# Gate matrix by two fp32r products per token, and one half of the context network's gate and up slabs split

## The chip, the cores and the metric

The kernel runs on one NeuronCore of one Trainium2 chip. The metric is device microseconds of one execution, and lower is better. The time before is the median of 3 runs.

## The reference, cut to what matters

The model is two blocks in a row. Its first ends with a product-key expert layer, and its second runs a stream of 512 tokens beside a context of 256 tokens, with modulated norms, mixers and gated feed-forward networks (silu of a gate times an up product, then a down product). The part that the change touches is this:

```python
experts = (i1 * PEER_NKEYS + i2).reshape(t, PEER_HEADS * PEER_TOPK)      # 128 of 16384 experts per token
gates = jax.nn.softmax(cv, axis=-1).reshape(t, PEER_HEADS * PEER_TOPK)
...
act = jax.nn.gelu(jnp.einsum('tkd,td->tk', expert_u[eb], xb))
out = jnp.einsum('tk,tkd->td', act * gb, expert_v[eb])
```

and, for the context, `(silu(x @ w_gate) * (x @ w_up)) @ w_down` with a hidden width of 22 slabs of 128.

## The kernel before, in words

**Products.** Most products are made in fp32r (a 32-bit format that TensorE takes in one pass) from an upper and a lower part of both operands: upper by upper, upper by lower, lower by upper, three products in place of one. ScalarE writes the upper part of a weight slab of 128x1024 (line 522), and VectorE or GpSimd the lower part (line 530), slabs in three buffers, at most two slabs ahead. A `direct` unit takes the slab and the activations whole in float32, one product per block of 128 rows (line 555, the first two slabs of a network at line 573); it needs no split, and no engine but TensorE.

**The context network** (`cnet`, class `Network`) handles 256 tokens. Its hidden width is in two halves of 11. Each half has 22 gate and up slabs and then 11 down slabs. All 66 slabs are direct. Its input comes from `cffn` (class `Apply`): VectorE scales 8 blocks, and ScalarE adds the shift to each (line 731, signal "moved").

**The dense gate matrix.** The first 384 tokens are handled densely: every expert slab is multiplied with all of them, and the gates of all other experts are zero. For each token, the 128x128 matrix of its gates is the product of two one-hot matrices over the token's 128 choices, one for each half of the expert number, one of them scaled by the gates. The stream `dense` works in 96 steps of GT = 4 tokens, and is three steps deep. In step k VectorE makes both one-hot matrices of tokens 4k to 4k+3 (line 3458), in the step after that ScalarE (4 operations, line 3469, even groups) or GpSimd (one operation, line 3486, odd groups) multiplies the gates in, and in step k+3 TensorE makes 4 float32 products of 128x128x128 (line 3443). ScalarE copies the result to a stage (line 3477), and the DMA queue of SyncE writes every fourth stage to DRAM (line 3494). Once all are written, the gates of each group of 8 slabs are loaded (`gates_sync`, line 3518). The dense steps need the chosen experts of their tile of 128 tokens, which the stream `route` finds on VectorE.

**The order** of the instructions on each engine is laid down when the kernel is built, by a planner (`Weave`). It keeps a clock for each engine, charges every operation a cost by a formula, and puts a step of a side stream in when the signals that its TensorE part needs are expected to have come and when the backlog of the engines that the step before used is over. The charges that matter here:

```python
if rhs.dtype == F32R:
    self.spent += max(n / 2400 + 0.013, 0.058)
else:
    self.spent += max(n * 0.00168, 0.14) * (1.0 if out.shape[0] > 64 else 0.55)
...
fixed, rate = {"vector": (0.14, 0.00106), "scalar": (0.14, 0.00089), "gpsimd": (0.35, 0.00205)}.get(self.name, (0, 0))
```

Where a stage ends with `plan.drain()`, all side steps that are left are put in before the spine goes on. After `cnet` come the 13 slabs of the context mixer `cm1` (split, lower parts on GpSimd), then such a drain, then `gates 1`, the start of the stream `experts`, and the 256 peer slabs of 384 tokens (split on ScalarE and VectorE).

**The experts stream** handles the last 128 tokens by fetching rows. GpSimd issues indirect DMAs (line 3646) of 128 rows of 4 KB into five buffers, VectorE multiplies and sums each (lines 3604 and 3618), in 257 steps that are due every 3.96 us of the planner's TensorE clock. The first step issues the first five fetches and holds the first VectorE operation. At the end TensorE transposes the sum (line 3593).

## Time and profile before

| | |
|---|---|
| median of 3 runs | 3975.88 us (3972.86 to 3977.01) |
| profiled execution, its own time | 3978.74 us |
| its span in the trace | 3976.9 us |
| granted TensorE clock, mean | 0.983 of 2.4 GHz |
| TensorE (PE) busy | 3823.1 us, 96% |
| VectorE (DVE) busy | 2328.4 us, 59% |
| ScalarE (ACT) busy | 1570.5 us, 39% |
| GpSimd (POOL) busy | 693.6 us, 17% |

Times are microseconds from the start of the span. Each float32 product stands in the trace as two records of PE and two of PEld (weight load), and each fp32r product as one of each. The duration of a PE record includes its latency, so what a product costs in a dense row of products is the distance from one start to the next. "us" of a merged row reaches from the first start to the last end.

### The profile page before, as it was taken

What the parts mean: (1) busy time and instruction counts of PE and PEld (TensorE: products, weight loads), DVE (VectorE), ACT (ScalarE), POOL (GpSimd) and SP (SyncE); (2) the same over time, 40 slices, a digit from 0 to 9 for tenths busy, and PEclk for the clock granted to TensorE, in tenths of its full rate; (3) what the DMA queues carried; (4) which work ended last, traced back from release to release, by engine and by line L of the source; (5) the groups of instructions that cost most, each with busy time, mean ns of one, the idle gap of its engine ahead of it and who ended that gap; (6) DMA issues with size and microseconds to landing.
All of it is one profiled execution on the core that took longest, in us unless ns stands there. A gap on an engine that the chain in (4) does not pass through costs nothing.

```text
span 3976.9 us, 55816 instructions
## 1 busy us (share of the span) xinstructions
PE 3823.1 (96%) x22529; PEld 3304.4 (83%) x22529; DVE 2328.4 (59%) x4053; ACT 1570.5 (39%) x2531; POOL 693.6 (17%) x586
## 2 busy tenths in 40 slices
PE   8999999989999989999999999998899999889998
PEld 5788776778899889999999999786677777667887
DVE  6455333546888467777777776557633345664333
ACT  4523342444345543333333333536522233564222
POOL 0112000244112343222233221201100010101000
PEclk9999999999999999999999999998999999999999
DMA  5211235533355678888888886312234342203332
GB/s 207 81 41 44 102 118 200 177 99 99 108 176 198 212 238 294 289 277 284 274 283 283 285 285 196 113 55 62 82 118 136 122 143 69 74 26 87 99 97 75
DMA packets 209184, 617.19 MB, mean 155 GB/s; under 512 B 18464, under 2 KB 68640, under 8 KB 205088
## 3 DMA queue, kind: packets, MB, share of 16 engines
q1 hardware_dynamic: 168352, 465.76, 36.6%
q0 software_dynamic: 40576, 147.87, 10.8%
q8 instruction: 179, 2.93, 0.3%
q14 instruction: 77, 0.63, 0.1%
HBM read 583.67 MB, written 29.88 MB: 154 GB/s over the span
## 4 chain that ended last, share of the span: by engine, by line
PE 85%; DVE 7%; ACT 4%; DMA 2%; issue 2%; POOL 0%; SPq 0%; DVEq 0%; ACTq 0%; POOLq 0%
PE ps L598 22%; PE ps L609 21%; PE ps L600 21%; PE ps L555 6%; PE ps L3443 2%; PE ps L2513 1%; DMA raw<-w_in 1%; PE ps L2540 1%; PE ps L887 1%; DVE hlo_plain L764 1%; ACT whi L522 1%; PE ps L2121 1%; PE ps L2531 1%; PE ps L1218 1%; PE ps L1209 1%
## 5 line engine op out<-in xcount | busy, mean ns | idle before, releaser
L598 PE MATMUL ps<-hhi,whi 128*128 128x512 f32 (+1 forms) x2824 | 1075.9, 381 | 6.8 <-DVE xres L3049 2.9
L600 PE MATMUL ps<-hlo,whi 128*128 128x512 f32 (+1 forms) x2824 | 1048.8, 371 | 0.1
L530 DVE TENSOR_TENSOR wlo<-raw,whi 128x1024 fp32r<-128x1024 f32 x543 | 671.3, 1237 | 635.6 <-ACT whi L522 628.2
L522 ACT ACTIVATE whi<-raw 128x1024 fp32r<-128x1024 f32 x594 | 625.7, 1054 | 601.7 <-PE ps L609 452.8
L609 PE MATMUL ps<-hhi,wlo 128*128 128x512 f32 (+1 forms) x2824 | 670.3, 376 | 9.0 <-DVE wlo L530 9.0
L598 PEld LDWEIGHTS ps<-hhi,whi 128*128 128x128 f32 x2824 | 532.9, 189 | 108.6 <-issue 25.4
L600 PEld LDWEIGHTS ps<-hlo,whi 128*128 128x128 f32 x2824 | 533.3, 189 | 68.8 <-issue 4.1
L609 PEld LDWEIGHTS ps<-hhi,wlo 128*128 128x128 f32 x2824 | 513.2, 189 | 83.7 <-DVE wlo L530 9.4
L600 PE MATMUL ps<-ag_lo,whi 128*128 128x384 f32 x1024 | 342.0, 334 | 0.0
L598 PE MATMUL ps<-ag_hi,whi 128*128 128x384 f32 x1024 | 342.0, 334 | 0.0
L3646 POOL DMA_INDIRECT fetched<-peer_v_rows,rows x128 | 151.3, 1182 | 359.9 <-DVE xtok L3618 335.7
L3646 POOL DMA_INDIRECT fetched<-peer_u_rows,rows x128 | 153.1, 1196 | 342.4 <-DVE ract L3604 325.5
L3530 ACT ACTIVATE uact<-ps 128x384 f32<-128x384 f32 x128 | 62.9, 491 | 362.0 <-PE ps L609 361.9
L609 PE MATMUL ps<-ag_hi,wlo 128*128 128x384 f32 x1024 | 198.2, 334 | 0.0
L600 PEld LDWEIGHTS ps<-ag_lo,whi 128*128 128x128 f32 x1024 | 192.3, 188 | 0.0
L598 PEld LDWEIGHTS ps<-ag_hi,whi 128*128 128x128 f32 x1024 | 192.2, 188 | 0.0
L609 PEld LDWEIGHTS ps<-ag_hi,wlo 128*128 128x128 f32 x1024 | 179.3, 188 | 0.0
L3604 DVE CUSTOM_DVE_ANT_0 fetched<-fetched,xtok 128x1024 f32<-128x1024 f32 x128 | 156.0, 1218 | 17.3 <-DMA fetched<-peer_u_rows,rows 17.3
L3618 DVE SCALAR_TENSOR_TENSOR xtok<-fetched,ract,xtok 128x1024 f32<-128x1024 f32 x127 | 162.4, 1279 | 0.0
L3547 DVE TENSOR_TENSOR uact<-uact,gin 128x384 f32<-128x384 f32 x128 | 71.4, 558 | 151.4 <-ACT uact L3530 146.0
L555 PE MATMUL ps<-hct_plain,raw 128*128 128x256 f32 x672 | 157.6, 379 | 0.0
L683 POOL COPY nacc<-nsq 128x512 f32<-128x512 f32 x6 | 3.7, 611 | 851.3 <-ACT nsq L672 851.3
(652 smaller groups left out, 6018.7 us busy)
## 6 DMA issues: line engine op xcount, KB each, us to landing
raw<-w_in SPq DMA_DIRECT2D x151, 512.0 KB
raw<-peer_u SPq DMA_DIRECT2D x128, 512.0 KB
raw<-peer_v SPq DMA_DIRECT2D x128, 512.0 KB
raw<-w_mod SPq DMA_DIRECT2D x96, 512.0 KB
raw<-w_gate SPq DMA_DIRECT2D x66, 512.0 KB
raw<-w_up SPq DMA_DIRECT2D x66, 512.0 KB
raw<-w_down SPq DMA_DIRECT2D x66, 512.0 KB
gate_dram<-stage SPq DMA_DIRECT2D x24, 1024.0 KB, 4.3
```

The source lines that it names most:

```text
L522: a.x.activation(whi[n % NW][:], raw[i % NRAW][:], ACT.Copy, bias=0.0, scale=1.0).then_inc(*a.gives("hi", i))
L530: e.x.tensor_tensor(wlo[n % NW][:], raw[i % NRAW][:], whi[n % NW][:].bitcast(F32), ALU.subtract).then_inc(*e.gives(*lo_sig(i)))
L555: ins = t.x.matmul(o, w[:, 128 * (first + k):128 * (first + k) + 128], p.plain, start=grp.opens and k == 0, stop=grp.closes and k == len(g ...
L598: t.x.matmul(o, w, p.hi, start=grp.opens and k == 0, stop=False)
L600: t.x.matmul(o, w, p.lo, start=False, stop=False)
L609: ins = t.x.matmul(o, lo[:, 128 * (starts[gi] + k):128 * (starts[gi] + k) + 128], p.hi, start=False, stop=grp.closes and k == len(grp.pair ...
L3443: ins = t.x.matmul(four(b, x), ea[n % 4][:, x, :], eb[n % 4][:, x, :], start=True, stop=True)
L3530: a.x.activation(uact[j % 2][:], held(("out", "peer_u", j))[:, 0:TD], ACT.Gelu_apprx_tanh, bias=0.0, scale=1.0).then_inc(*a.gives("peer_a" ...
L3547: v.x.tensor_tensor(t3, t3, gin[g % 2][:, :, jj, :], ALU.mult).then_inc(*v.gives("peer_v", "gated", j))
L3604: v.x.tensor_tensor_reduce(c[:], c[:], xtok[:], 1.0, 0.0, ALU.mult, ALU.add, ract[:, i:i + 1]).then_inc(*v.gives("expert_v", "dot", i))
L3618: v.x.scalar_tensor_tensor(xtok[:], c[:], ract[:, i:i + 1], xtok[:], ALU.mult, ALU.add).then_inc(*v.gives("expert_v", "sum", i))
L3646: g.x.indirect_dma_start(fetched[i % NF][:], None, io["peer_v_rows" if i >= 128 else "peer_u_rows"], bass.IndirectOffsetOnAxis(ap=rows[:, ...
```

## The change

Part one, the dense gates. The gates of a tile are split into an upper part in fp32r (`gThi`) and a lower part (`gT`) when they arrive. The one-hot matrices are fp32r. The second one-hot matrix is multiplied by the upper and by the lower gates: GpSimd makes the lower product for all 96 steps and the upper product for every second step, ScalarE the upper product of the other steps (one step later than before, and after GpSimd's lower product). TensorE makes two fp32r products per token, both with the first one-hot matrix as weights. There are three buffers of the lower products.

Part two, the context network. `cffn` makes, beside the whole activations, an upper part (8 copies on ScalarE) and a lower part (8 subtractions on GpSimd). The 22 gate and up slabs of the second half are split (upper on ScalarE, lower on GpSimd), the first half and all down slabs stay direct. The hidden parts lie elsewhere.

Part three, the stream `experts` gets one step more, ahead of the first: the first fetches are issued in it, and the next step is due 14 us later.

```diff
@@ Apply
+            for c, p in enumerate(self.pairs if self.apart else []):
+                a.wait_ge("apply_a", self.name, "moved", c)
+                a.x.activation(p.hi, p.plain, ACT.Copy, bias=0.0, scale=1.0).then_inc(*a.gives("apply_a", self.name, "hi", c))
...
+            if self.apart:
+                g.wait_ge("apply_v", self.name, "made", KC - 1)
+                g.wait_ge("route_t", "scores", 15)
+                for c, p in enumerate(self.pairs):
+                    g.wait_ge("apply_a", self.name, "hi", c)
+                    g.x.tensor_tensor(p.lo, p.plain, p.hi.bitcast(F32), ALU.subtract).then_inc(
+                        *g.gives("apply_g", self.name, "lo", c))
@@ Network
-                        u = Unit(kind, (self, k), io[w][l * 22 + k], n, [Group(pairs, (self, k))], ring, lo[half])
+                        u = Unit(kind, (self, k), io[w][l * 22 + k], n, [Group(whole if self.direct and half == 0 else pairs, (self, k))],
+                                 ring, lo[half])
+                        u.direct = self.direct and half == 0
@@ best_pairs, last step of a tile
-            v.x.tensor_copy(gT[:, ts], b[:, 256:384]).then_inc(*sig("tile", n))
+            v.x.tensor_copy(gThi[n], b[:, 256:384]).then_inc(*sig("gates upper", n))
+            after("gates upper", n)
+            v.x.tensor_tensor(gT[:, ts], b[:, 256:384], gThi[n].bitcast(F32), ALU.subtract).then_inc(*sig("tile", n))
@@ dense_tensor
                 for x in range(GT):
-                    ins = t.x.matmul(four(b, x), ea[n % 4][:, x, :], eb[n % 4][:, x, :], start=True, stop=True)
+                    t.x.matmul(four(b, x), ea[n % 4][:, x, :], eb[n % 4][:, x, :], start=True, stop=False)
+                    ins = t.x.matmul(four(b, x), ea[n % 4][:, x, :], lower[n % 3][:, x, :], start=False, stop=True)
@@ dense_scalar
-            if 1 <= k <= NQ and k % 2:
-                a.wait_ge("dense_v", k - 1)
+            if 2 <= k <= NQ + 1 and k % 2 == 0:
+                e = eb[(k - 2) % 4]
+                a.wait_ge("dense_v", k - 2)
+                a.wait_ge("dense_g", k - 2, "lower")
                 for x in range(GT):
-                    n = GT * (k - 1) + x
-                    ins = a.x.activation(ea[(k - 1) % 4][:, x, :], ea[(k - 1) % 4][:, x, :], ACT.Copy, bias=0.0, scale=gT[:, n:n + 1])
-                ins.then_inc(*a.gives(*gated(k - 1)))
+                    n = GT * (k - 2) + x
+                    ins = a.x.activation(e[:, x, :], e[:, x, :].bitcast(F32), ACT.Copy, bias=0.0, scale=upper_gates(n, 1))
+                ins.then_inc(*a.gives(*gated(k - 2)))
@@ dense_gpsimd
-            if 1 <= k <= NQ and k % 2 == 0:
-                e = ea[(k - 1) % 4]
+            if 1 <= k <= NQ:
+                e = eb[(k - 1) % 4]
                 g.wait_ge("dense_v", k - 1)
-                g.x.tensor_tensor(e, e, along(gT[:, GT * (k - 1):GT * k]), ALU.mult).then_inc(*g.gives(*gated(k - 1)))
+                if k >= 4:
+                    g.wait_ge("dense_t", k - 4)
+                g.x.tensor_tensor(lower[(k - 1) % 3], e.bitcast(F32), along(gT[:, GT * (k - 1):GT * k]), ALU.mult).then_inc(
+                    *g.gives("dense_g", k - 1, "lower"))
+                if k % 2 == 0:
+                    g.x.tensor_tensor(e, e.bitcast(F32), along(upper_gates(GT * (k - 1), GT)), ALU.mult).then_inc(
+                        *g.gives(*gated(k - 1)))
@@ experts
     def expert_tensor(t):
+        yield Every(14.0)
         for i in range(257):
             yield Every(3.96)
...
     def expert_vector(v):
+        yield
...
         for i in range(NF - 1):
             fetch(i)
+        yield
@@ the network of the context
-    cnet = Network(0, 1, TC, cffn.pairs, list(range(145, 152)) + list(range(168, 185)), "clate", ("vector", "gpsimd"), [], ("up", "down"))
+    cnet = Network(0, 1, TC, cffn.pairs, list(range(168, 181)), "clate", ("vector", "gpsimd"), [], cffn.whole)
```

## Rows read from the trace of the kernel before

**Rows 1.** Page, part 4: the chain that ended last, by engine.
```profile
PE 85%; DVE 7%; ACT 4%; DMA 2%; issue 2%; POOL 0%; SPq 0%; DVEq 0%; ACTq 0%; POOLq 0%
```

**Rows 2.** Busy time by stretch around the change; the last columns are clock, DMA share, GB/s.
```profile
core 0: us, PE busy (x) PEld busy (x) DVE busy (x) ACT busy (x) POOL busy (x), PEclk, DMA share, GB/s
1062.00:1372.00 310.00, 310.00 (x1816) 282.59 (x1814) 239.18 (x477) 143.50 (x342) 60.76 (x56) 1.00 0.58 192
1372.00:1433.00 61.00, 51.73 (x373) 49.22 (x372) 33.09 (x54) 35.65 (x60) 31.50 (x17) 0.92 0.52 155
1433.00:1461.00 28.00, 18.95 (x100) 18.64 (x101) 10.52 (x16) 7.07 (x10) 9.87 (x8) 0.88 0.88 304
1461.00:2500.00 1039.00, 1039.00 (x5999) 1038.93 (x5998) 785.57 (x1013) 370.19 (x512) 302.99 (x256) 1.00 0.83 274
```

**Rows 3.** Busy time by stretch of the one-hot matrices' own instructions alone.
```profile
1088.00:1196.00 108.00, 30.57 (x232) 30.46 (x232) 38.74 (x32) 20.31 (x64) 16.92 (x16) 1.00 0.56 182
1196.00:1321.00 125.00, 56.30 (x428) 56.17 (x429) 64.21 (x53) 33.11 (x105) 28.87 (x27) 1.00 0.60 205
```

**Rows 4.** PE in order of time: a dense step, direct slabs, the next dense step.
```profile
1122.08 1.05 PE L3443 MATMUL ps<-onehot 128*128 128x128 f32 x8
1122.97 3.19 PE L555 MATMUL ps<-hct_plain,raw 128*128 128x256 f32 x14
1126.00 1.05 PE L3443 MATMUL ps<-onehot 128*128 128x128 f32 x8
```

**Rows 5.** PE in order of time: fp32r products of 256 columns.
```profile
1387.57 1.12 PE L609 MATMUL ps<-hchi,wlo 128*128 128x256 f32 x8
1388.53 0.28 PE L598 MATMUL ps<-hchi,whi 128*128 128x256 f32 x1
```

**Rows 6.** PE in order of time: fp32r products of 128 columns, then one of 256.
```profile
2797.96 0.39 PE L2513 MATMUL ps<-l_skd,l_sqs 128*128 128x128 f32 x2
2798.19 0.28 PE L2513 MATMUL ps<-l_rskd,l_sqs 128*128 128x256 f32 x1
```

**Rows 7.** PE in order of time: float32 records of 64 columns, weights of 128x128.
```profile
2607.43 1.00 PE L2141 MATMUL ps<-l_qin,l_Sen 128*128 128x64 f32 x8
2608.24 0.47 PE L598 MATMUL ps<-hhi,whi 128*128 128x512 f32 x1
```

**Rows 8.** Groups by line and shape: busy us, mean ns, idle before.
```profile
L530 POOL TENSOR_TENSOR wlo<-raw,whi 128x1024 fp32r<-128x1024 f32 x52 | 126.4, 2443 | 130.3 <-ACT whi L522 126.1 <-PE ps L609 4.2
L3469 ACT ACTIVATE onehot<-onehot,gT 128x128 f32<-128x128 f32 x192 | 60.8, 390 | 5.1 <-DVE onehot L3458 4.6
L3486 POOL TENSOR_TENSOR onehot<-onehot,gT 128x512 f32<-128x512 f32 x48 | 52.0, 1084 | 236.8 <-DVE onehot L3458 236.7
L522 ACT ACTIVATE whi<-raw 128x1024 fp32r<-128x1024 f32 x594 | 625.7, 1054 | 601.7 <-PE ps L609 452.8 <-DMA raw<-w_in 70.2 <-DMA raw<-w_down 19.0
```

**Rows 9.** DVE in order of time while POOL splits slabs, in `cm1`.
```profile
1394.41 0.69 DVE L2271 SCALAR_TENSOR_TENSOR c_tmp<-c_tmp,c_C 128x512 f32<-128x512 f32 x1 [3.37 <-ACT c_C L2202]
1396.44 2.71 DVE L2278 TENSOR_TENSOR c_tmp<-c_C 128x512 f32<-128x512 f32 x1
```

**Rows 10.** PE, DVE and POOL in order of time at the start of the experts.
```profile
1436.09 1.55 PE L609 MATMUL ps<-hhi,wlo 128*128 128x384 f32 x8
1440.25 1.55 PE L609 MATMUL ps<-hhi,wlo 128*128 128x384 f32 x8
1441.70 1.05 POOL L3646 DMA_INDIRECT fetched<-peer_u_rows,rows  x1 [10.39 <-issue]
1451.19 1.23 DVE L3604 CUSTOM_DVE_ANT_0 fetched<-fetched,xtok 128x1024 f32<-128x1024 f32 x1 [17.28 <-DMA fetched<-peer_u_rows,rows]
1453.61 2.93 PE L609 MATMUL ps<-hhi,wlo 128*128 128x384 f32 x8 [9.04 <-DVE wlo L530]
1456.34 0.49 PE L598 MATMUL ps<-hhi,whi 128*128 128x384 f32 x1
```

**Rows 11.** SP's issues in order of time: the first two gate loads.
```profile
1384.16 0.38 SPq L3518 DMA_DIRECT2D gin<-gate_dram  x1
1440.87 0.38 SPq L3518 DMA_DIRECT2D gin<-gate_dram  x1
```

**Rows 12.** The stage's writes to DRAM, and the last expert sum's instructions.
```profile
DMA to landing us min/median/max: 3.8/4.3/5.8
2453.33 1.28 DVE L3618 SCALAR_TENSOR_TENSOR xtok<-fetched,ract,xtok 128x1024 f32<-128x1024 f32 x1
2475.25 1.55 PE L609 MATMUL ps<-ag_hi,wlo 128*128 128x384 f32 x8
```

More of the change, by code:

```diff
@@ L770, in vector @@
                         yield
-            for c in [] if self.only else range(3, KC) if self.once else [KC - 1]:
+            for c in [] if self.apart else range(3, KC) if self.once else [KC - 1]:
                 self.lower_vector(v, c)
         def gpsimd(self, g):
-            if self.once:
-                for c in range(0 if self.only else 3):
+            if self.apart:
+                g.wait_ge("apply_v", self.name, "made", KC - 1)
[4 more added lines that the diff above has]
+                        *g.gives("apply_g", self.name, "lo", c))
+            elif self.once:
+                for c in range(3):
                     p = self.pairs[c]
@@ L3068, in program, with __init__ @@
     class Network:
-        def __init__(self, l, v, n, pairs, places, ring, lo, free, direct=()):
+        def __init__(self, l, v, n, pairs, places, ring, lo, free, whole=None):
             self.l, self.v, self.n, self.free, nm = l, v, n, free, f"f{v}{l}"
-            self.name, self.direct = nm, direct
-            self.whole = [sb(f"{nm}w{k}", places[2 * k], [n])[:] for k in range(HALF)] if "down" in direct else None
-            self.hid = [[sb(f"{nm}h{k}{y}", places[2 * k + y], [n], F32R)[:] for y in range(2)] for k in range(HALF)]
-            self.sg = [sb(f"{nm}sg{i}", places[2 * HALF + i], [n])[:] for i in range(2)]
-            self.taken = "lo" if v and not self.whole else "up"
+            self.name, self.direct = nm, whole is not None
+            inner = len(places) - 2
+            self.plain = [sb(f"{nm}plain{k}", places[k], [n])[:] for k in range(HALF)] if whole else None
+            self.hid = [[sb(f"{nm}h{k}{y}", places[2 * k + y], [n], F32R)[:] for y in range(2)] for k in range(HALF)] if not whole else None
+            self.sg = [sb(f"{nm}sg{i}", places[inner + i], [n])[:] for i in range(2)]
             self.units = []
@@ L3092, in __init__ @@
                             groups.append(Group([], (self, half, o), k == 0, False))
-                        if self.whole:
-                            groups[-1].pairs.append(Pair(None, None, ("ffn_v", nm, "up", HALF * half + k), None, self.whole[k]))
+                        if self.direct:
+                            groups[-1].pairs.append(Pair(None, None, ("ffn_v", nm, "up", HALF * half + k), None, self.plain[k]))
                         else:
@@ L3107, in fgate_scalar @@
         if k >= 2:
-            a.wait_ge("ffn_v", f.name, "up" if f.whole else "lo", k - 2)
+            a.wait_ge("ffn_v", f.name, "up" if f.direct else "lo", k - 2)
         for s in f.free:
@@ L3115, in product @@
     def product(f, k):
-        return f.whole[k % HALF] if f.whole else held(("out", "fup", (f, k)))[:, 0:f.n] if f.v else f.sg[k % 2]
+        return f.plain[k % HALF] if f.direct else held(("out", "fup", (f, k)))[:, 0:f.n] if f.v else f.sg[k % 2]
     def fup_vector(v, i, phase):
@@ L3124, in fup_vector @@
             v.wait_ge("ffn_a", f.name, "gate", k)
-            if f.whole and k >= HALF:
+            if f.direct and k >= HALF:
                 v.wait_ge(*last_of("fdown", (f, 0, (7 * HALF + k - HALF) // 8)))
             v.x.tensor_tensor(c, held(("out", "fup", (f, k)))[:, 0:f.n], f.sg[k % 2], ALU.mult).then_inc(*v.gives("ffn_v", f.name, "up", k))
-        elif not f.whole:
+        elif not f.direct:
             v.wait_ge("ffn_a", f.name, "hi", k)
@@ L3134, in fup_scalar @@
         f, k = spine[i].key
-        if phase and not f.whole:
+        if phase and not f.direct:
             a.wait_ge("ffn_v", f.name, "up", k)
@@ L3427, in gated @@
     def gated(k):
[L3429 removed]
+        return ("dense_g", k, "upper") if k % 2 else ("dense_a", k, "gated")
     def dense_tensor(t):
@@ L3630, in expert_scalar @@
     def expert_scalar(a):
-        for i in range(128):
+        for i in range(129):
             yield
```

28 lines of the change are left out of this document (16 added, 12 removed).

## The prediction

> **What bounds the kernel now.** I read four views. The page's chain of work that ended last comes first: TensorE makes up 85% of it [rows 1], so a change is worth what it takes from TensorE, unless another engine comes to hold it up. Next, the busy times by stretch [rows 2]. The context network (1062 to 1372) has TensorE busy for all of its 310 us, beside a VectorE at 239 and a GpSimd at 61. In the context mixer after it (61 us) TensorE idles for 9.3 us. At the start of the peer slabs (28 us) it idles for 9.1 us, and after that it is busy throughout. Third, the timeline of TensorE, for the distance between products [rows 4 to 7]. Fourth, the timeline around 1433 to 1461 [rows 10]. The reader is to see two things: that the network's stretch is TensorE's alone, and that the one long wait near it belongs to the experts' start.
>
> **Slabs of the second half.** A direct product of 256 columns is two records. 14 records fill the 3.03 us from 1122.97 to 1126.00, so a record takes 0.216 us and a product 0.433 [rows 4]. A direct slab of 8 products is 3.46 us. An fp32r product of 256 columns takes 0.96 us / 8 = 0.12 us [rows 5], and a split slab of 24 of them 2.88. Over 22 slabs that is 22 x (3.46 - 2.88) = 12.9 us less. The splits are 22 x 1.05 us on ScalarE and 22 x 2.44 us on GpSimd (53.7 us) [rows 8]. ScalarE has room: it is busy for 143.5 of 310 us [rows 2]. `cffn`'s 8 copies and 8 subtractions start behind the whole activations, and the first half needs neither. I cost them at nothing, because some 100 us of direct products cover them. Without that cover they would be some 10 us.
>
> **The dense products.** A dense step of 4 tokens takes 0.89 us of TensorE now [rows 4]. The change makes 8 fp32r products of 128 columns of it. Two such products stand together in one place of the trace: 0.23 us to the start of the next, so 0.115 each [rows 6]. That is hardly less than the 0.12 of 256 columns [rows 5], so their columns don't set it. In rows 7 float32 records of only 64 columns, with weights of 128x128, fill 0.81 us with 8, some 0.10 each. I read both as the time of one weight load, which the fp32r product of 128 columns can't hide. Eight of them are 0.81 to 0.92 us, against 0.89: over 96 steps -8 to +3 us. The rows with the right format are those at 0.115, so I take +1.4. The float32 saving that the change seems to promise is not there.
>
> The Trainium skill bears on this, on the page "TensorE: Matmul & The Clock Gate". Its section "LDWEIGHTS (loading the stationary operand)" gives a load as the weight's columns over 1.2 GHz, 107 ns for 128 columns. With that a step would be 0.86 us and the 96 steps -3 us. The trace agrees within 8 ns (0.115). The section "Back-to-back issue gap" gives an isolated product of 128 columns 134 cycles, 56 ns, and would make a step 0.45 us and the 96 steps -42 us. That is the rule by which the change would pay most, and it is a rival below.
>
> **GpSimd, the new load.** Per step it had half an operation of 1.08 us, and now has one and a half: 1.63 us [rows 8]. ScalarE keeps its 4 operations of 0.39 us per two steps. VectorE gets three small copies, 1 us in all. Of the 96 steps, 32 lie ahead of the second half and 53 inside its 125 us of gate and up slabs [rows 3]. There GpSimd would now need 53.7 + 53 x 1.63 = 140 us, where TensorE needs 63.4 + 53 x 0.905 = 111. So GpSimd can't keep up, and the dense steps slide back. How far, is a question of order. The planner charges GpSimd 0.35 + 512 x 0.00205 = 1.40 us for an operation that takes 1.08, so 2.10 per step, and TensorE 0.53 for a step. It admits steps while GpSimd's time lasts: by its charges (63 - 54) / 1.57 = 6 steps in the stretch, by the rows (63.4 - 53.7) / 0.72 = 13. I take 10. In the 11 down slabs (38 us, some 10 us of GpSimd taken by the norm's sums and the next splits) it is 18 by the charges and 38 by the rows. I take 20. In `cm1` GpSimd is busy for 31.5 of 61 us already [rows 2], which leaves some 12 steps. That is 42 of 64, and 22 are left at the drain ahead of the peer slabs, where TensorE does nothing else.
>
> A step there costs GpSimd's 1.63 us and not TensorE's 0.905, so 0.72 more: 22 x 0.72 = +15.8 us. Bounds: none left, 0, and 45 left, +32. Steps that land in `cm1` fill some of TensorE's waits. Of the 9.3 us idle there I take -3. GpSimd's operations also stretch VectorE's: one of two like operations took 2.71 us and the other 0.69, while GpSimd split slabs [rows 9]. I take +1.
>
> **The experts' start.** VectorE's first dot product stood in its queue at 1433.9, waited 17.3 us for its row, and behind it lay the lower parts of the slabs [rows 10]. TensorE waited 9.04 us for one of these. The groups at line 609 are 4.16 us apart, so the one at 1453.61 is 9.2 us late, and the next slab starts 2.73 us after it where 1.39 is usual: 10.5 us lost. The change holds the first dot product back by 14 us of products, to some 1448, with the row there at 1451. VectorE may be held up for 3 us, and before it took 10 us of that until TensorE stood still. So -10.5 us. At the other end the experts finish 14 us later: the last sum is at 2453.3 and the slabs behind the drain that waits for them begin some 1.4 us after 2475 [rows 12], so some of the 14 us is covered and a transpose may wait: +1, bound +4.
>
> What is late next is the gate load. It was issued at 1384, 52 us ahead of the first peer groups [rows 10, 11]. With 22 steps left at the drain it is issued 5 us after the last dense product (4.3 us for the stage's write [rows 12]), together with the second gate load and five fetches. VectorE then waits for it at the first peer slab, with the lower parts behind. I take +3, bounds 0 and +10.
>
> **Sum.** -12.9 + 1.4 + 15.8 - 3 + 1 - 10.5 + 1 + 3 = -4.2 us. On the profiled execution (3978.74 us, 1.8 above its span) that is 3974.5. On the median of the runs, 2.9 us lower, it is 3971.7, and I say 3972. About 0.2% (8 us) is what a measurement here can tell from no change.
>
> **Rivals.**
> A, the tail hides. If GpSimd's slack, which the rows show and the charges don't, lets nearly all dense steps end in `cm1`, the terms of 15.8 and 3 go: 3953. For it speaks that GpSimd's whole need from 1196 on (54 + 64 x 1.63 + 31 = 189 us) is less than the 237 us there. Against it is that the order is laid down by the charges.
> B, the other side: the tail is long. If the charges rule everywhere (6 + 18, and 2 in a `cm1` whose splits leave GpSimd little), 38 to 42 steps are left, 12 to 14 us more than I took, and the gate load comes when all else does, 5 more. That is +14, or 3990. It decides from 28 steps left (even) and 39 left (0.2% slower).
> C, columns set the time of fp32r at 128 as they do from 256 to 384. From 0.12 by another half, 0.067 us each, a step is 0.53 us, and the 74 steps that are not in the drain give back 28 us: 3944. Against it stand rows 6 and 7. The skill's gap of 56 ns is this case.
> D, the wait at the experts' start stays, because VectorE waits for gates in place of a row. It costs 10.5 us again: 3982. For it speaks that both loads and the fetches share one burst, at 304 GB/s already [rows 2].
>
> **Chances.** My forecast, 3962 to 3982, 0.36; A 0.24; B 0.24; C 0.08; D 0.08. Faster takes A, C and 0.10 of mine, 0.42. Within 0.2% takes 0.26 of mine and 0.06 of D, 0.32. Slower takes B and the rest, 0.26. The range runs from C's time to B's with the gate load at its bound: 3945 to 3998.
>
> **What would show it.** Right: dense products at line 3443 0.11 to 0.12 us apart; split slabs of the second half 2.9 us apart; VectorE's one-hot operations still running after 1385; a stretch before the peer slabs with TensorE busy only half the time, in groups 1.6 us apart; no wait of 9 us behind the first fetch. Wrong: dense groups at 0.5 us (C), or the last dense step before 1400 (A). The likeliest error is the number of steps left at the drain, at 0.72 us each.

## The result and the profile after

The changed kernel takes 4011.0 us (median of 4 runs, 4007.1 to 4015.1) where the kernel before takes 3976.5 beside it: a ratio of 1.0085, with a 95% interval of 1.0074 to 1.0097. That is 34.6 us slower. The prediction was 3972 us in a range of 3945 to 3998, and slower had a chance of 0.26. The time lies 13 us above the range. In the profiled executions the span went from 3976.9 to 4007.1 us, 30.2 more.

The busy time by stretch of the changed kernel comes first; its columns are those of [rows 2].

```profile
1200.00:1280.00 80.00, 69.37 (x551) 68.37 (x550) 74.47 (x137) 39.65 (x71) 62.31 (x35) 0.94 0.50 161
1420.00:1440.00 20.00, 19.06 (x85) 18.27 (x86) 12.63 (x11) 11.90 (x31) 15.46 (x16) 0.50 0.37 151
1440.00:1460.00 20.00, 19.06 (x86) 18.27 (x86) 11.86 (x10) 12.35 (x34) 16.01 (x17) 0.50 0.36 147
1480.00:1500.00 20.00, 15.48 (x74) 15.48 (x75) 14.19 (x21) 7.96 (x14) 5.03 (x3) 0.74 0.89 278
```

Three places are new. Between 1200 and 1280, where TensorE never idled before, it now idles for 10.6 us. From 1420 to 1460 only dense steps run, and the granted clock is 0.50, the lower of TensorE's two levels (1.2 GHz). From 1480 to 1500 it idles again. TensorE's waits from 1055 to 1560 name the releasers (total, times, longest):

```profile
PE ps L3210 <- DVE hlo_plain L768: 10.0, 3, 7.6
PE ps L598 <- ACT uact L3561: 6.6, 1, 6.6
PE ps L598 <- ACT c_nvT L1991: 5.1, 1, 5.1
PE ps L628 <- ACT hchi L738: 3.4, 1, 3.4
...
PE ps L2119 <- DVE c_tmp L2297: 1.9, 1, 1.9
```

Before, the one long wait was that of 9.0 us at line 609, on the lower part of a slab [rows 10]. It is gone. A wait of 6.6 us for `uact` (the activations of a peer slab, which ScalarE writes) stands near its place. New are 10 us of waits for `hlo_plain`, the input of the transposes of `H1`. `H1` is the `Apply` that makes the input of the peer slabs; its operations on VectorE wait for the router's last tile.

A dense step, by TensorE's timeline: first one at the high clock in the last mixer, then two pieces of the drain ahead of the peer slabs.

```profile
1403.91 0.28 PE L3465 MATMUL ps<-onehot 128*128 128x128 f32 x1
1404.02 0.28 PE L3466 MATMUL ps<-lower,onehot 128*128 128x128 f32 x1
1404.13 0.28 PE L3465 MATMUL ps<-onehot 128*128 128x128 f32 x1
...
1410.81 0.45 PE L3465 MATMUL ps<-onehot 128*128 128x128 f32 x1
...
1414.64 0.45 PE L3465 MATMUL ps<-onehot 128*128 128x128 f32 x1 [0.19 <-ACT onehot L3494]
1414.88 0.41 PE L3466 MATMUL ps<-lower,onehot 128*128 128x128 f32 x1
1415.10 0.41 PE L3465 MATMUL ps<-onehot 128*128 128x128 f32 x1
...
1418.47 0.45 PE L3465 MATMUL ps<-onehot 128*128 128x128 f32 x1 [0.19 <-ACT onehot L3494]
...
1464.08 0.63 PE L598 MATMUL ps<-hhi,whi 128*128 128x384 f32 x1
```

At the high clock the products are 0.11 us apart, 0.89 for the 8 of a step. In the drain they are 0.213 apart, and two steps take 3.83 us (1414.64 to 1418.47). The drain lasts from 1410.81 to the first peer product at 1464.08: 53.3 us for the 28 steps that stand there in the order of instructions, 1.90 each.

The start of the experts, VectorE and then SyncE in order of time:

```profile
1482.97 0.56 DVE L3578 TENSOR_TENSOR uact<-uact,gin 128x384 f32<-128x384 f32 x1 [15.75 <-DMA gin<-gate_dram]
1488.77 1.22 DVE L3637 CUSTOM_DVE_ANT_0 fetched<-fetched,xtok 128x1024 f32<-128x1024 f32 x1
```
```profile
1441.94 23.32 SPq L3525 DMA_DIRECT2D gate_dram<-stage  x4
1471.16 7.85 SPq L3549 DMA_DIRECT2D gin<-gate_dram  x2
1479.05 8.07 SPq L514 DMA_DIRECT2D raw<-peer_u  x3
```

VectorE no longer waits for the fetched row of the first dot product. It idles for 15.75 us until the gates are there. The first `uact` was written at 1470.1, so the last 12.9 us are the gates' alone. Both gate loads, 57 us apart before [rows 11], go out together here, and three weight loads stand behind them.

**The account.** I measure the start of the peer slabs by ScalarE's first `uact`: 1437.67 before, 1469.61 after, 31.9 us later. From there to the end it is 2539.2 us before and 2537.5 after, 1.7 less. Together that is the 30.2. Three marks split each span further: the first product of the context network, the first `uact` and the last.

| kernel | start to network | network to first `uact` | first to last `uact` | last `uact` to end |
|---|---|---|---|---|
| before | 1053.7 | 384.0 | 1035.0 | 1504.2 |
| changed | 1049.7 | 419.9 | 1032.9 | 1504.6 |
| e1 | 1050.1 | 383.7 | 1023.3 | 1505.1 |
| e2 | 1047.0 | 380.4 | 1023.3 | 1509.0 |
| e3 | 1052.8 | 422.1 | 1034.6 | 1504.2 |
| e4 | 1050.2 | 405.2 | 1033.2 | 1505.0 |
| e5 | 1047.9 | 419.8 | 1028.1 | 1509.4 |
| e6 | 1047.2 | 388.7 | 1031.4 | 1510.1 |
| e7 | 1051.9 | 356.9 | 1031.5 | 1510.8 |
| e9 | 1051.3 | 422.1 | 1033.0 | 1507.6 |
| e10 | 1051.2 | 422.2 | 1023.4 | 1507.5 |
| e12 | 1049.6 | 373.6 | 1023.4 | 1505.1 |
| e13 | 1052.4 | 404.6 | 1031.3 | 1510.4 |
| e14 | 1051.5 | 378.8 | 1023.4 | 1510.5 |

The changed kernel, e3, e5, e9 and e10 have one order of instructions up to the peer slabs. In the first column they still differ by 4.9 us, in the second by 2.4. The last column, which no edit aims at, has 6.6 us between its ends. So effects are read from the two middle columns, and only where they are clear of some 2 us. The change costs 35.9 us in the second and gives back 2.1 in the third. Its profile happened to reach the network 4.0 us earlier, which is why the spans differ by 30.2 and the medians by 34.6.

The 35.9 are made of -12.9 (split slabs; two of them start at 1202.94 and 1205.82, 2.88 us apart), +10.0 (`hlo_plain`), +28 x (1.90 - 0.89) = +28.3 (drain), +1.7 (`c_nvT`, 5.1 against 3.4) and +0.4 (`c_tmp`): 27.5, with 8.4 us left. Most of that is what a wait costs beyond its length. Behind the wait of 7.6 us the products run at the low clock first:

```profile
1247.38 0.45 PE L3210 MATMUL ps<-cst,hlo_plain 128*128 128x128 f32 x1 [7.61 <-DVE hlo_plain L768]
1249.12 0.41 PE L600 MATMUL ps<-c0apart,whi 128*128 128x256 f32 x1
1249.34 0.41 PE L598 MATMUL ps<-hchi,whi 128*128 128x256 f32 x1
...
1254.09 0.28 PE L598 MATMUL ps<-hchi,whi 128*128 128x256 f32 x1
1254.21 0.28 PE L600 MATMUL ps<-c0apart,whi 128*128 128x256 f32 x1
```

They are 0.21 us apart up to 1251.3 and 0.12 behind it. The mean granted clock is 0.94 from 1200 to 1280 and 0.96 from 1280 to 1372, and was 1.00 in both. That is 80 x 0.06 + 92 x 0.04 = 8.5 us of full clock, less the 1.6 that only the kernel before lost in its mixer (0.98 and 0.94 from 1400 to 1440). So some 7 us of the 8.4 is my estimate, an upper one, since part of it falls on idle time. The experiments take the rest apart.

### The profile page after: what moved, and what is told of

It is laid out like the page before. It is cut to its first block, busy times and chain, and to the rows that moved or that the text cites. A ratio compares the mean times of both kernels' runs of the same rounds, so it can differ in the third digit from the quotient of the medians.

```text
span 4007.1 us, 56544 instructions
## 1 busy us (share of the span) xinstructions
PE 3839.3 (96%) x22705; PEld 3327.2 (83%) x22705; DVE 2355.8 (59%) x4056; ACT 1591.1 (40%) x2561; POOL 844.8 (21%) x712
## 4 chain that ended last, share of the span: by engine, by line
PE 83%; DVE 8%; ACT 4%; issue 2%; DMA 2%; POOL 0%; SPq 0%; DVEq 0%; ACTq 0%; POOLq 0%
PE ps L598 22%; PE ps L609 21%; PE ps L600 21%; PE ps L555 4%; PE ps L2524 1%; PE ps L898 1%; PE ps L3465 1%; PE ps L3466 1%; DVE hlo_plain L768 1%; DMA raw<-w_in 1%; PE ps L2551 1%; ACT whi L522 1%; PE ps L2132 1%; PE ps L2542 1%; PE ps L1229 1%
## 5 line engine op out<-in xcount | busy, mean ns | idle before, releaser
L522 ACT ACTIVATE whi<-raw 128x1024 fp32r<-128x1024 f32 x616 | 648.9, 1055 | 599.9 <-PE ps L609 445.8
L530 POOL TENSOR_TENSOR wlo<-raw,whi 128x1024 fp32r<-128x1024 f32 x74 | 180.9, 2456 | 144.6 <-ACT whi L522 144.6
```

The costliest lines, as they stand in the source:

```text
L522: a.x.activation(whi[n % NW][:], raw[i % NRAW][:], ACT.Copy, bias=0.0, scale=1.0).then_inc(*a.gives("hi", i))
L530: e.x.tensor_tensor(wlo[n % NW][:], raw[i % NRAW][:], whi[n % NW][:].bitcast(F32), ALU.subtract).then_inc(*e.gives(*lo_sig(i)))
```

## Experiments

Medians are given with the ratio to runs of the kernel before on the same chip and its 95% interval. "Peer start" is the time of the first `uact`, and "rest" is the span less that time. "Slab time" is the third column of the table, from the first to the last `uact`.

**e1: the experts' hold alone.** Into the kernel before:

```
     def expert_tensor(t):
+        yield Every(14.0)
...
     def expert_vector(v):
+        yield
```

> The kernel before with the third part of the change alone: the first fetch and the first dot product of the experts are held back by 14 us of products. Theory: nothing but the wait behind the first dot product goes, 10.5 us, so 3966 us, with VectorE's wait for the first row under 4 us and the gates long there. Rival: the wait only changes its name (a row that is late again, or gates), 3976 us.

3966.1 us, 0.9974 (0.9964 to 0.9985). Rest: 2528.4 us against 2539.2 before, 10.8 less. The slab time is 1023.3 against 1035.0, 11.7 less. TensorE has no wait above 0.3 us between the last mixer and 1560, and VectorE waits 1.85 us for its first row:

```profile
1447.23 1.23 DVE L3606 CUSTOM_DVE_ANT_0 fetched<-fetched,xtok 128x1024 f32<-128x1024 f32 x1 [1.85 <-DMA fetched<-peer_u_rows,rows]
```

The term of -10.5 us was right, where the gates are there early.

**e2: slabs and hold, dense products as before.** The changed kernel with the dense functions of the kernel before.

> Parts two and three of the change without part one: the second half's gate and up slabs are split, the experts are held back, the dense products stay float32 with one product per token. Theory of the changed kernel's trace: GpSimd's splits of 2.4 us stretch VectorE's short operations and so bring the wait of 10 us at H1's transposes by themselves: 3976.5 - 12.9 + 10 - 10.5 = 3963 us, and the dense steps end ahead of the last mixer as before, so VectorE finds the gates there. Rival: the wait at H1 came from VectorE's queue behind the new dense steps; then it is gone here and the time is 3953 us. Second rival: splitting alone slides dense steps to the drain, 3975 us or more.

3964.0 us, 0.9967 (0.9956 to 0.9979). Peer start is 1427.37 against 1433.79 in e1, but the network also began 3.1 us earlier. From the network to the first `uact` it is 380.4 us against 383.7: the split slabs bring 3.3 us, and by the medians 2.1, where the intervals overlap. So the 12.9 us that TensorE saves on them are nearly all lost again. Up to the last mixer's first wait (1362.88 and 1374.05) 8.1 us of them are there, after 4.4 us of idle TensorE between 1200 and 1280. Another 4.8 go in the mixer, where one wait is 1.5 longer and the clock 0.83 from 1400 to 1420, against 1.00 in e1. No dense step is left at the drain. The time is what the theory gave, but not for its reason: the waits on VectorE at the transposes come to 3.5 us here, not to 10.

**e3: slabs and dense products, no hold.**

> The changed kernel without its third part: the experts start as in the kernel before. Theory: in the changed kernel the gates, not the row, are what VectorE waits for at the start of the peer slabs, so that the hold of 14 us buys nothing there: 4011 us, as with it. Rival: the hold brings its 10.5 us and the changed kernel lost them elsewhere; then this is 4021 us.

4015.9 us, 1.0100 (1.0084 to 1.0115), 5 us above the changed kernel and between the two expectations. Its slab time is 1034.6 against 1032.9, so at the experts' start the hold brings 1.7 us here, where in e1 it brought 11.7. The other 5.3 us lie ahead of the peer start, where the hold is not at work; kernels with one order of instructions up to there (the changed one, e3, e5, e9, e10) had their peer start anywhere from 1467.7 to 1474.9.

**e4: dense products and hold, all slabs direct.**

> Parts one and three of the change without part two: dense products in fp32r with split gates, the experts held back, the second half's gate and up slabs direct as before. In this order of instructions 8 dense steps are left at the drain, against 28 in the changed kernel. Theory: a drained step costs about 1.9 us at a fallen clock where a hidden one costs 0.9, so the drain adds 8 us, the dearer product 2, a short wait for the gates 3, and the hold gives 10.5: 3979 us. Rival: the dense products themselves cost more, wherever they stand; then this comes close to the changed kernel, 4000 us or more.

3995.4 us, 1.0047 (1.0033 to 1.0061): 16 above the theory, 5 below the rival. Peer start is 21.6 us later than in e1. TensorE's waits in that stretch (the last mixer's is 6.2 against 3.4 in e1):

```profile
PE ps L598 <- ACT uact L3551: 6.8, 1, 6.8
PE ps L598 <- ACT c_nvT L1981: 6.2, 1, 6.2
PE ps L628 <- ACT whi L522: 4.4, 1, 4.4
...
PE ps L3455 <- ACT onehot L3484: 3.1, 5, 1.3
PE ps L630 <- POOL wlo L530: 1.9, 1, 1.9
```

The mixer's first products wait for their splits (4.4 + 1.9), and its chain is 2.8 longer. The 8 drained steps take 14.2 us (1435.22 to 1449.39), 7.1 more than hidden ones, and 1.4 of the 3.1 us for `onehot` lie ahead of them: 17.6 of 21.6. The slab time is 1033.2, 9.9 above e1, though only 8 steps were drained. So the dense part alone takes back most of the hold's gain, and it makes the mixer wait. The drain of e4 begins at the high clock, and shows two drained steps at it, and then at the low one:

```profile
1435.22 0.30 PE L3455 MATMUL ps<-onehot 128*128 128x128 f32 x1 [0.85 <-ACT onehot L3484]
1438.67 0.30 PE L3455 MATMUL ps<-onehot 128*128 128x128 f32 x1 [1.29 <-ACT onehot L3484]
1442.11 0.45 PE L3455 MATMUL ps<-onehot 128*128 128x128 f32 x1 [0.19 <-ACT onehot L3484]
1445.94 0.45 PE L3455 MATMUL ps<-onehot 128*128 128x128 f32 x1 [0.19 <-ACT onehot L3484]
```

The first two take 3.45 us, 1.72 each, with TensorE waiting 1.29 for ScalarE's gated matrix. At the low clock they take 3.83. So of the 1.0 us that a drained step costs more than a hidden one, only some 0.2 is the low clock, as far as this one pair shows. No wait at `H1` shows here: between 1200 and 1280 TensorE is busy all 80 us. That wait needs the split slabs too.

**e5, e9, e10: what is late at the peer slabs.** In e5 and e10 the first 8 peer slabs multiply by `uact` itself:

```
+            if g:
+                v.wait_ge(f"gin{g % 2}", g)
+            v.x.tensor_tensor(t3, t3, gin[g % 2][:, :, jj, :] if g else t3, ALU.mult)
```

In e9 and e10 the second gate load moves behind two weight loads:

```
     plan.start("experts", streams["experts"])
-    run(GJ)
+    run(2)
+    plan.put("do", "gates", 1)
+    run(GJ - 2)
```

> The changed kernel, in which the first 8 peer slabs multiply their activations by themselves and not by the gates (their gating is left out); the gate load is still issued, but nothing waits for its first part. Theory: after the first peer slab the changed kernel takes 2537.5 us and the kernel before with the hold alone 2528.4; these 9 us are VectorE's wait for the late gate load, so 4002 us and no wait of TensorE above 2 us at the start of the peer slabs. Rival: the row of the first dot product, the fetches or the fallen clock make them up; then the time stays at 4009 to 4011.

4008.1 us, 1.0080 (1.0063 to 1.0097), and a rest of 2537.5 us, that of the changed kernel to the tenth. That equality is chance: the slab time is 1028.1, 4.8 us less, and what follows the last `uact` is 4.8 longer. So without the wait for gates half of the loss stayed. ScalarE shows what came in its place:

```profile
1480.17 0.49 ACT L3561 ACTIVATE uact<-ps 128x384 f32<-128x384 f32 x1 [2.31 <-PE ps L609]
1489.41 1.06 ACT L522 ACTIVATE whi<-raw 128x1024 fp32r<-128x1024 f32 x1 [8.76 <-DMA raw<-peer_u]
```

A weight slab is 8.76 us late; it stood in SyncE's queue behind both gate loads. TensorE waits 2.9 us in place of 6.6.

> The changed kernel with one edit of order: the second gate load is issued after the second peer slab and not right behind the first, so two weight loads of 512 KB go out ahead of it in SyncE's queue. In the changed kernel both gate loads, 1.5 MB each, went out together at 1471.16 and filled 7.9 us of that queue, and without any wait for gates the weights still came 8.8 us late. Theory: the first gate load has the DMA engines to itself and the weights follow sooner; 9 us are lost there in all, and the order gives back 4 to 6: 4006 us. Rival: the first load alone, issued behind the last dense product, takes its 12 us whatever follows it; 4011 us.

4015.1 us, 1.0088 (1.0073 to 1.0103), slab time 1033.0. The rival holds: VectorE idles for 15.76 us until its gates are there, and TensorE's wait of 6.6 us for `uact` is as long as in the changed kernel.

> The edits of e5 and e9 together: the first 8 peer slabs are not gated by the loaded gates (left out), and the second gate load goes out after two weight loads. Theory: the late first gates and the weights queued behind the two loads are two waits that cover each other, either of which costs the 9 us; with both gone TensorE waits under 2 us at the start of the peer slabs: 4002 us. Rival: the burst of fetches, weights and gates is the limit in any order; then the time stays at 4006 or more.

4005.8 us, 1.0068 (1.0052 to 1.0083). On the same chip that is 9.3 us below e9, clear of both ranges. TensorE is busy all through 1480 to 1500, and the slab time is 1023.4 us, 9.5 less than in the changed kernel and that of e1:

```profile
1480.00:1500.00 20.00, 20.00 (x117) 20.00 (x117) 13.02 (x21) 8.73 (x14) 2.95 (x3) 1.00 1.10 349
```

So the late drain makes two waits that overlap: VectorE's for the gates, which costs 9.6 us of slab time, and ScalarE's for a weight slab behind the two gate loads, which costs 4.8 when it stands alone (e5). Taking away the weights' wait alone gives nothing (e9), the gates' alone half, and both the whole 9.6. The 9.6 are the idle 6.6 us and 16 products at the low clock behind it, 0.32 us apart in place of 0.17, with 8 more that are slow in part.

**e6, e7: TensorE's load against GpSimd's.** Both leave the lower gate parts out of the sum. e6 drops the second product alone, e7 also GpSimd's operation that makes it:

```
-                    t.x.matmul(four(b, x), ea[n % 4][:, x, :], eb[n % 4][:, x, :], start=True, stop=False)
-                    ins = t.x.matmul(four(b, x), ea[n % 4][:, x, :], lower[n % 3][:, x, :], start=False, stop=True)
+                    ins = t.x.matmul(four(b, x), ea[n % 4][:, x, :], eb[n % 4][:, x, :], start=True, stop=True)
```

> The changed kernel without the second product of each token (the part of the gates below their upper half is left out of the sum); GpSimd still makes it. 32 steps stand in the drain by the order of instructions. Theory: in the drain GpSimd now sets the pace at 1.63 us per step and TensorE, with 4 products, does not; hidden steps cost 0.46. So 64 x 0.46 + 32 x 1.63 = 81.6 us of steps against 68 x 0.9 + 28 x 1.88 = 113.8 in the changed kernel, 32 less: 3979 us. Rival: TensorE alone set the pace; then a drained step falls to some 1.25, VectorE's operation, and the time to 3967.

3980.9 us, 1.0008 (0.9999 to 1.0018). TensorE and GpSimd in its drain:

```profile
1422.35 1.94 PE L3465 MATMUL ps<-onehot 128*128 128x128 f32 x8 [1.06 <-ACT onehot L3493]
1425.34 1.94 PE L3465 MATMUL ps<-onehot 128*128 128x128 f32 x8 [1.05 <-ACT onehot L3493]
```
```profile
1400.00:1420.00 20.00, 12.62 (x53) 11.51 (x53) 16.02 (x14) 15.30 (x42) 20.00 (x21) 0.50 0.38 158
```

Two steps take 2.99 us, and GpSimd is busy for 20.00 of 20 us. So GpSimd needs 1.50 us per step (three operations of 1.0 us for two steps), not the 1.63 that I had. In the changed kernel TensorE, busy for 19.06 of 20 us at 1.90 per step, was the slower of the two.

> The changed kernel without the lower part altogether: neither GpSimd's operation that makes it nor the second product (both left out of the sum). GpSimd's load is that of the kernel before, half an operation per step, beside the split slabs. 16 steps stand in the drain. Theory: GpSimd's new operation causes the slide and the wait of 10 us at H1: 80 x 0.46 + 16 x 1.3 = 58 us of steps against 113.8, the wait at H1 down to 4, and gates that are there in time: 4011 - 56 - 6 - 5 = 3944 us. Rival: the slide comes from the split slabs' GpSimd work alone; then the wait at H1 is still 10 us and the time 3960 or more.

3950.4 us, 0.9928 (0.9912 to 0.9945). 16 steps are left at the drain instead of 32, and TensorE's waits for `hlo_plain` fall from 7.8 us in e6 to 1.2. Against e6 that is 30 us for one GpSimd operation per step, with the same work on TensorE. This was nearest to the test of the main idea, and it holds in part: GpSimd's new operation makes half of the slide of e6 and nearly all of its wait at `H1`. It does not make the other half. With GpSimd's dense load that of the kernel before, 16 steps still slid to the drain, where e2 has none, and the slab time is 1031.5, 8.2 above e1. Nor do those steps run faster. Between 1380 and 1400 GpSimd is busy for 7.64 us only, and ScalarE's copies of every second step's result are still 2.98 us apart:

```profile
1380.00:1400.00 20.00, 13.48 (x56) 12.34 (x56) 15.80 (x15) 14.82 (x41) 7.64 (x8) 0.50 0.60 247
```
```profile
1392.95 0.60 ACT L3499 ACTIVATE stage<-ps 128x512 f32<-128x512 f32 x1 [0.74 <-PE ps L3464]
1395.93 0.60 ACT L3499 ACTIVATE stage<-ps 128x512 f32<-128x512 f32 x1 [0.74 <-PE ps L3464]
```

No engine is full there; each waits for the next one. Which of the change's other parts slides these 16 steps, and what sets their pace, was not tested.

**e8: does a busy TensorE get its clock back?** From step 70 on:

```
+                for x in range(2 if n >= 70 else 0):
+                    t.x.matmul(b.rearrange("p (v j) -> p v j", v=4), ea[n % 4][:, x, :], ea[n % 4], start=True, stop=True)
```

> The changed kernel with two more products of 512 columns ahead of the 8 of each dense step from step 70 on (their result is overwritten); the order of the rest is as in the changed kernel, 28 steps in the drain. Theory: TensorE runs the drain at the granted clock of 0.50 because its products of 128 columns leave it half idle, and its own pace of 1.88 us per step is that of the low clock. The filler brings the clock to 1.00, where a step's products take 0.89 + 0.43 us, under GpSimd's 1.63: 28 x (1.88 - 1.63) = 7 us less, 4004 us. Rival: the clock stays low whatever TensorE does there; then a step takes 1.88 + 0.85 and the time is 4035.

4030.9 us, 1.0130 (1.0114 to 1.0147). The rival holds:

```profile
1420.00:1440.00 20.00, 20.00 (x80) 18.45 (x80) 9.80 (x8) 9.43 (x24) 12.30 (x12) 0.50 0.26 108
1440.00:1460.00 20.00, 20.00 (x80) 18.45 (x79) 9.80 (x8) 9.43 (x24) 12.30 (x12) 0.50 0.26 106
```

TensorE doesn't idle, yet the granted clock stays at 0.50, and the filler costs its full price at 1.2 GHz. The theory's premise was wrong too: in the changed kernel's drain TensorE is not half idle but busy for 19.06 of 20 us. The Trainium skill, page "TensorE: Matmul & The Clock Gate", section "What's actually happening", has the full clock come back once TensorE has been busy for a while; by the busy time of the profile this run doesn't agree. At the peer slabs behind the drain the clock does come back. What tells the two stretches apart stays open: the filler, like the dense step, multiplies one-hot matrices, nearly all zeros, so the run separates neither the shape nor the content of the products from their number.

**e11, e12, e14: the length of GpSimd's splits.** One edit, in the changed kernel (e11) and in e2 (e12; in e14 with 2 parts):

```
+        parts = 4 if e.name == "gpsimd" and spine[i].kind in ("fgate", "fup") else 1
+        w = 1024 // parts
+        for q in range(parts):
+            c = slice(w * q, w * q + w)
+            ins = e.x.tensor_tensor(wlo[n % NW][:, c], raw[i % NRAW][:, c], whi[n % NW][:, c].bitcast(F32), ALU.subtract)
```

> The changed kernel with GpSimd's split of each gate and up slab (one operation of 1024 columns, 2.4 us) cut into four operations of 256 columns, as much work in all; 26 dense steps stand in the drain against 28. Theory: VectorE's short operations that ran 2.4 us in place of 0.3 waited out one whole operation of GpSimd, and the wait of 10 us at H1's transposes is made of these; in quarters they wait out 0.6 us: TensorE's wait at H1 falls under 4 us, and with two drained steps less the time is 4011 - 7 - 2 = 4002 us. Rival: it is GpSimd's total work, not the length of one operation, that holds up VectorE; then the wait at H1 stays near 10 and the time above 4008.

4009.2 us, 1.0074 (1.0058 to 1.0089), no different from the changed kernel, and one wait of 8.8 us for `hlo_plain` remains. But VectorE's operations show the mechanism. First the changed kernel, then e11, the same instructions of the router:

```profile
1215.07 3.58 DVE L3366 TENSOR_SCALAR su<-ciu 128x128 uint32<-128x128 uint32 x3
1218.68 2.39 DVE L3368 SCALAR_TENSOR_TENSOR rank<-su 128x128 f32<-128x128 uint32 x1
1221.11 2.36 DVE L3370 SCALAR_TENSOR_TENSOR rank<-su,rank 128x128 f32<-128x128 uint32 x1
```
```profile
1209.27 2.15 DVE L3372 TENSOR_SCALAR su<-ciu 128x128 uint32<-128x128 uint32 x3
1211.45 0.72 DVE L3374 SCALAR_TENSOR_TENSOR rank<-su 128x128 f32<-128x128 uint32 x1
1212.21 0.71 DVE L3376 SCALAR_TENSOR_TENSOR rank<-su,rank 128x128 f32<-128x128 uint32 x1
...
1231.88 6.92 DVE L3417 TENSOR_TENSOR chosen<-chosen,ksm 128x128 f32<-128x128 f32 x1
```

In the kernel before, the two `rank` operations take 0.29 us each. Beside GpSimd's splits of 2.4 us they take 2.4, beside quarters of 0.7 us they take 0.7: each lasts as long as one operation of GpSimd. The Trainium skill, page "SBUF — State Buffer", section "SBUF: two separate sides", says that the two engines share a pair of ports by an exclusive lock, which an operation holds for its whole length. That agrees with these rows. The last row it leaves open: the operation at 1231.88 took 6.92 us, to the end of a stretch in which GpSimd ran eight quarters and two dense operations without a gap (1231.04 to 1238.64). What lets VectorE in between two operations of GpSimd, or not, stays open.

> The kernel of the second run (split slabs and held experts, dense products in float32 as before) with GpSimd's splits of gate and up slabs in quarters. There TensorE idled 4.4 us between 1200 and 1280. Theory: most of that goes with the quarters: 3964 - 3 = 3961 us. Rival: it stays, 3964, or the four starts of an operation cost GpSimd so much that splits come late: 3968.

3955.5 us, 0.9945 (0.9932 to 0.9959), the fastest kernel of this study that computes everything. TensorE idles 3.1 us between 1200 and 1280, where it was 4.4 in e2, and its waits there for VectorE are gone. Peer start is 1423.20, 4.2 earlier than in e2. From the network to the first `uact` it is 373.6 us, 6.8 less than in e2 and 10.1 less than in e1, so here the split slabs pay most of their 12.9.

> The kernel of e12 with GpSimd's splits of gate and up slabs in halves of 512 columns (1.2 us) and not in quarters. Theory: what VectorE's short operations wait out is one operation of GpSimd, so halves keep most of the gain: 3958 us, between 3964 with whole splits and 3955.5 with quarters. Rival: it is the order of instructions that the quarters happened to get, and not the length; then halves give 3964, as the whole splits, whose order they have.

3964.5 us, 0.9953 (0.9940 to 0.9967). By the median the rival holds, but the intervals of the ratios of e12 and e14 overlap. The idle time between 1200 and 1280 is 2.9 us, no more than with quarters. So the gain of quarters over halves, if there is one, isn't in that stretch. It lies in the last mixer: from its first wait to the first `uact` it is 64.5 us in e2, 66.6 in e14 and 59.5 in e12. TensorE waits there 4.9 us for `c_res` in e2 and e14 and 3.5 for `c_nvT` in e12. Whether quarters or the order that they bring did that was not separated.

**e13: the changed kernel, with the planner's charges as measured.**

```
-            self.spent += max(n / 2400 + 0.013, 0.058)
+            self.spent += 0.111 if n == 128 else max(n / 2400 + 0.013, 0.058)
...
-        self.spent += fixed + rate * width(out)
+        self.spent += 1.08 if self.name == "gpsimd" and list(out.shape) == [128, 4, 128] else fixed + rate * width(out)
```

> The changed kernel with two of the planner's charges set to what the trace shows: 1.08 us for a GpSimd operation of a dense step in place of 1.40, and 0.111 us for an fp32r product of 128 columns in place of 0.066. No instruction changes, only the order; 8 steps stand in the drain against 28. Theory: a drained step costs 1.92 us and one among slabs 0.89, so 20 steps give 20 x 1.03 = 20.6 us back, and part of the 9 us of late gates goes too: 3987 us. Rival: GpSimd really can't carry those steps among the slabs; then TensorE waits for its gates there, and the time stays at 4005 or more.

3994.4 us, 1.0036 (1.0023 to 1.0049): 16.6 below the changed kernel, with the same instructions in another order. The start of its drain, of 8 steps:

```profile
1434.74 0.65 PE L2403 MATMUL ps<-cst,c_svT 128*128 128x128 f32 x2
1435.88 0.45 PE L3465 MATMUL ps<-onehot 128*128 128x128 f32 x1 [0.49 <-ACT onehot L3494]
1439.71 0.45 PE L3465 MATMUL ps<-onehot 128*128 128x128 f32 x1 [0.19 <-ACT onehot L3494]
```

Two drained steps still take 3.83 us. From the network to the first `uact` it is 15.3 us less than in the changed kernel (20 steps x 1.0 would be 20), and the slab time is 1031.3, 8.0 above e1: the gates and weights are nearly as late behind a drain of 8 steps as behind one of 28. TensorE still idles 11.6 us between 1200 and 1280. So most of the long drain was a matter of order, but steps put among the slabs bring other waits.

## Why the prediction was wrong

**The step that failed is the tail: 22 steps left at the drain, at 0.72 us each, +15.8 us.** The place and the kind of loss were right: dense steps slid back to where TensorE does nothing else. Both factors were too small. The number is 28 and the price 1.90 - 0.89 = 1.01 us, so the term measured 28.3. I priced a drained step by GpSimd's 1.63 us and took TensorE's 0.905 at the high clock for granted. The drain runs at a granted clock of 0.50, where TensorE's own 8 products take 1.71 us and a step 1.90; GpSimd needs 1.50 (e6). Two steps at the high clock (e4) took 1.72 each, also above 1.63, because the engines wait for each other. So the price was short by 0.1 us for that and by 0.2 for the clock. The clock should have been a factor: [rows 2] show it lower (0.92 and 0.88) wherever TensorE idles, and the late group of [rows 10] shows what that costs (2.73 us to the next slab in place of 1.39). Rival B, with 38 to 42 steps at 0.72 and 3990 us, had the right sign by the wrong factor.

**Slabs, -12.9: right as TensorE's own saving** (2.88 us a slab), and wrong as a gain. The splits bring waits and a lower clock that the prediction put at nothing, and by themselves (e2 against e1) leave some 3 us. With quarters (e12) 10.1 are left.

**The price of fp32r at 128 columns, +1.4: right within 2 us.** They are 0.111 us apart at the high clock. I had read 0.115, which gives 0.92 a step and +2.9 over 96 steps, and took 0.905 and +1.4. Rival C (0.067) falls. A step of two fp32r products per token costs what the float32 one did, 0.89.

**Contention, +1: wrong by an order.** I had seen an operation of 2.71 beside one of 0.69 us [rows 9] and counted one such case, in the mixer. The change puts 22 splits of 2.4 us beside the router's short VectorE operations, a chain that TensorE waits for at `H1`. Where dense steps also load GpSimd (the changed kernel, e6, e11) TensorE idles for 10 to 15 us between 1200 and 1280; with slabs alone (e2) for 4.4; with the dense part alone (e4) not at all. That VectorE's stretched operations make these waits fits the rows of e11, and e7, where most of the wait goes with GpSimd's operation, but no run isolates it. e11 shows that the length of a single operation is not the whole of it: cut in four, the wait at `H1` was still 8.8 us.

**Gaps of the last mixer filled, -3: wrong.** The wait for `c_nvT` grew from 3.4 to 5.1 us, and to 6.2 in e4, with dense steps in the mixer. That VectorE's and ScalarE's dense operations stand ahead of the mixer's is my reading, and not shown.

**The experts' start, -10.5: right by itself (e1, 11.7), and undone by the next term.** Late gates were +3 with bounds 0 and +10, and are +9.6 (slab time 1032.9 against 1023.3), near the upper bound. I had named the gate load, the second one that goes out with it, and the shared burst. I had not seen that the two fill SyncE's queue for 7.9 us with weights behind them, which costs half of it even without the gates (e5, e10). Rival D, that the wait at the experts' start stays at its price of 10.5 because VectorE waits for gates, was right on this point. The +1 at the other end doesn't show: 1504.6 us from the last `uact` against 1504.2.

The misses add up: 12.5 (drain), some 9 (contention), 5 (mixer) and 6.6 (gates) are 33 of the 38.8 us between -4.2 and +34.6. No term had the lower clock behind the new waits, at most some 7 us, which covers the other 6.

## What to carry to other kernels

Price work that slides out of cover by what it will find there, not by what it had: here a step went from 0.89 to 1.90 us, some 0.8 of it because the engines wait for each other and some 0.2 for the low clock (one pair of steps in e4). Price a new wait above its length: the products behind it ran at the low clock for another 4 us or more. When an engine with slack gets long operations, list the short operations of the engine beside it that something waits for. When a dependent stage gets later, look at the whole queue behind its first transfer: of two waits that overlap, removing one shows less than it costs, or nothing. And where a planner lays out the order, give it measured prices before judging a change: e13's two numbers were worth 16.6 us, though the change still loses. What pays is the rest of it, without the dense part: the hold (e1), and the split slabs with quarters (e12); with whole splits (e2) they hardly pay.

## What the runs showed of the hardware

- TensorE fully busy at the lower clock for 60 us did not get the higher one back (e8), with 8 products of 128 columns and 2 of 512 per step; at the slabs of 384 columns behind it the clock came back. All products of that stretch were of one-hot matrices, so their content isn't ruled out.
- An fp32r product of 128 columns with new weights takes 0.111 us at the high clock and 0.213 at the low one (one of 256 columns 0.12 and 0.21), so what bounds it doubles as the clock halves. The Trainium skill, page "TensorE: Matmul & The Clock Gate", section "LDWEIGHTS (loading the stationary operand)", gives the weight's columns over 1.2 GHz for a load, 107 ns here, and names no clock state; it fits the first and not the second.
- A wait of TensorE of 7.6 us was followed by products 0.21 us apart for 4 us, and by the same ones 0.12 apart after that; one of 6.6 us by 16 products 0.32 apart in place of 0.17.
- A short VectorE operation lasted as long as one GpSimd operation beside it (2.4 or 0.7 in place of 0.29 us), and once as long as what was left of an unbroken run of ten (6.92 us).
- Two gate loads of 1.5 MB, issued back to back, held SyncE's queue for 7.9 us. In e9 the first one alone took 0.38, but then the two weight loads of 512 KB behind it took 13.5.
